# First mixer in another order: rotations and compression beside the attention gate's slots, a weight slot in each attention unit, pool output split, tanh gates

## The chip, the cores and the metric

One core of a Trainium2 chip. The metric is the device time of one execution in microseconds. The kernel before took 3319.39 us, the median of 3 runs (3317.85 to 3319.66).

## The reference, cut to what matters

Two transformer blocks on 256 tokens of width 2048, all in float32. The change is mostly in the first block's mixer:

```python
h = rmsnorm(x, norm_w)
proj = h @ w_in
(u_pool, g_pool, q, kc_raw, vc_raw, k_sel, v_sel, k_win, v_win, g_nsa, g_br) = split(proj)
y_pool = pool_mixer(u_pool, pool_mix, pool_scale) * silu(g_pool)   # causal means over 2, 4, 8, 16 tokens
y_a = y_pool @ w_pool_out
qh = rope(heads(q, 16), pos)
kc = rope(compress(heads(kc_raw, 4), pe_k, w1_k, w2_k), cmp_pos)   # 15 blocks of 32 tokens, stride 16:
vc = compress(heads(vc_raw, 4), pe_v, w1_v, w2_v)                  #   silu(block . w1) . w2, hidden 256
ksh, kwh = rope(heads(k_sel, 4), pos), rope(heads(k_win, 4), pos)
gates = sigmoid(g_br)
o_nsa = nsa_attention(qh, kc, vc, ksh, v_sel, kwh, v_win, gates)   # three softmaxes per head, gated, summed
y_b = (o_nsa * silu(g_nsa)) @ w_nsa_out
gm = sigmoid(h @ w_merge + b_merge)                                # 2 x 2048 wide
x = x + (gm[0] * y_a + gm[1] * y_b) @ w_out
```

The second block has its own input projection (with three narrow row projections ff, mi, mf), a forgetting attention, an mLSTM cell, an output projection and a PEER layer with 16384 experts, whose weights are most of what is loaded.

## The kernel before

**Weights as a stream of slots.** All large weights lie in one DRAM tensor `stream`, cut in slots of 128 x 2048 floats (1 MB). SyncE loads slot after slot into `raw[0]` and `raw[1]` in turn, each as soon as `raw_free` says that it may. A float32 product is made of three fp32r products: ScalarE rounds the slot, `whi <- raw` (`split`, L865), VectorE makes the rest, `wlo <- raw - whi` (L1343), which also frees `raw`, and TensorE multiplies whi by the high part of the activations (hTh), whi by the low part (hTl), and wlo by hTh. In `phase_t2` the first two are one matmul of 512 columns and VectorE adds the two halves as it reads the bank (`evac_t`, L1371); in `t_slot` (L431) there are 48 matmuls of 256 columns per slot; in `phase_n` (L497) 24 of 512 columns, and the tokens lie on partitions. A slot can be rounded only when the slot two before it has been multiplied (`slot_used`), and the split of slot n+1 runs under the matmuls of slot n. `phase(..., ahead=True)` also splits the first slot of what follows; elsewhere the next phase splits its first slot after its predecessor's last bank has been read.

**PHASES** gives the order of the stages in units of 4 slots: in_t 16 (u, g_pool, kc_raw, vc_raw, k_sel, k_win, q, g_nsa), in_n 2 (v_sel, v_win), narrow1 0.5 (g_br: 48 columns, stored 128 wide in one slot, and a dummy slot), cmp 2 (w1_k, w1_v), merge 8, pool_out 2, nsa_out 4, out1 4, then the second block.

**Between in_n and the attention** TensorE waits for both slots of narrow1, turns the gates, and then multiplies the cmp slots straight from `raw` in fp32 (L539, out 128 x 60, weights the stationary side, 256 matmuls in all). ScalarE takes the silus of g_pool and g_nsa at once (L944, L945) and swaps halves for the rotations (L952, L953), 12 pairs of heads; VectorE builds `kb` (L1423) and multiplies and adds the rotations (L1433 to L1435). GpSimd has pooled `u` during in_t (L1274 to L1290).

**The attention** has 32 units, u = 16 heads x 2 query blocks. TensorE's order is: turn(u) (L578, L580), scores(u+2) (L564 to L566), perhaps one t_slot of merge, values(u) (L589, L593). turn waits for VectorE's scaling (L1467), scores for ScalarE's copy of the turned probabilities (L982, L983), because both use banks 4 to 7. On VectorE: mask(u+1), scale(u), split. On ScalarE: exp(u+1) (L973, L974), copy(u), split, sigmoid of a merge bank (L992). Twenty of the 32 units have a slot (`MERGE_AT`); a sigmoid between exponentials has a table load on either side.

**After it**: the pooled groups are mixed (z, L621), 12 merge slots follow, then pool_out straight from `raw` in fp32 (L635, 16 matmuls per slot), gates on VectorE (L1521); before it the branch's 8 high parts (L1028) and low parts (L1514), 16 nsa_out slots with gate and sum (L1531, L1533), again 8 high and 8 low parts, and out1. `narrow2` (L506) in the second block is made like narrow1, followed by in2_v and in2_m.

## Time and profile before

| | us |
|---|---|
| median of 3 runs | 3319.39 |
| profiled execution | 3320.34 |
| its span | 3318.6 |
| matmul busy | 3073.2 |
| VectorE, ScalarE, GpSimd busy | 1758.4, 1244.0, 39.8 |

Loaded and written: 542.25 MB, 163 GB/s over the span. Mean granted TensorE clock 0.954. The page's chain of work that ended last is 82% TensorE, 11% VectorE and 5% ScalarE. The views used below are the page, tables of stretches, single rows of the timeline of one engine, groups of instructions by line, and the answer for one source line. Times are from the start of the span.

### The profile page before, as it was taken

To read this page: it belongs to the slowest core of one execution; us is meant where nothing else is said; L and a number is where in the kernel's file an instruction comes from. 1 tells how busy PE (TensorE), PEld (TensorE's weight loads), DVE (VectorE), ACT (ScalarE), POOL (GpSimd) and SP (SyncE) were. 2 spreads that over 40 slices of the span, in tenths; PEclk is the share of its full clock that TensorE was granted. 3 is DMA by queue.
4 is the path that set the end of the run, shared out by engine and by line. 5 is a ranking of instruction groups with operands and counts; after the bars stand their busy time and mean duration, and the time that the engine had idled before them with its cause. 6 is when DMAs were issued, how large, how long until landed. Compare 5 with 4: busy or idle time off the path is not lost.

```text
span 3318.6 us, 46264 instructions
## 1 busy us (share of the span) xinstructions
PE 3073.2 (93%) x18679; PEld 2750.7 (83%) x18679; DVE 1758.4 (53%) x2398; ACT 1244.0 (37%) x1352; POOL 39.8 (1%) x31
## 2 busy tenths in 40 slices
PE   6999998889998698995899999989999999999997
PEld 6888887778997587874689999988888999988885
DVE  4555453444244544566547988864445354444444
ACT  3333344444223333333334344434443333334443
POOL 0400000000000000000000000000000000000000
PEclk9999977989999898997999999999999999999998
DMA  4555543223454344431354445545555855545554
GB/s 178 187 181 188 177 152 115 77 77 115 153 185 160 123 177 152 153 127 64 139 181 165 174 165 171 164 158 190 190 191 194 276 185 182 184 164 191 190 190 152
DMA packets 89854, 542.25 MB, mean 163 GB/s; under 512 B 9264, under 2 KB 25648, under 8 KB 25904
## 3 DMA queue, kind: packets, MB, share of 16 engines
q1 hardware_dynamic: 71824, 522.33, 44.3%
q10 hardware_dynamic: 17952, 18.88, 1.7%
q8 instruction: 49, 0.80, 0.1%
q14 instruction: 29, 0.24, 0.0%
HBM read 530.68 MB, written 10.49 MB: 163 GB/s over the span
## 4 chain that ended last, share of the span: by engine, by line
PE 82%; DVE 11%; ACT 5%; issue 1%; DMA 0%; ACTq 0%; DVEq 0%; SPq 0%
PE bank L431 25%; PE bank L829 21%; PE bank L452 10%; PE bank L497 8%; PE bank L450 6%; DVE wlo L1343 4%; PE bank L473 3%; ACT whi L865 2%; PE bank L635 2%; PE bank L539 2%; DVE R L1883 1%; PE bank L449 1%; DVE R L1327 1%; PE bank L593 1%; PE bank L564 1%
## 5 line engine op out<-in xcount | busy, mean ns | idle before, releaser
L1343 DVE TENSOR_TENSOR wlo<-raw,whi 128x2048 fp32r<-128x2048 f32 x476 | 1090.0, 2291 | 796.9 <-ACT whi L865 795.6
L865 ACT ACTIVATE whi<-raw 128x2048 fp32r<-128x2048 f32 x476 | 908.2, 1910 | 1018.5 <-PE bank L452 368.2
L431 PE MATMUL bank<-hT,whi 128*128 128x256 f32 x5888 | 1116.3, 291 | 14.1 <-DVE wlo L1343 12.5
L431 PEld LDWEIGHTS bank<-hT,whi 128*128 128x128 f32 x5888 | 933.5, 196 | 18.4 <-issue 10.0
L431 PE MATMUL bank<-hT,wlo 128*128 128x256 f32 x2944 | 842.8, 286 | 0.0
L431 PEld LDWEIGHTS bank<-hT,wlo 128*128 128x128 f32 x2944 | 573.6, 195 | 0.0
L452 PE MATMUL bank<-hT,whi 128*128 128x512 f32 x1440 | 517.4, 401 | 0.0
L450 PE MATMUL bank<-hT,wlo 128*128 128x256 f32 x1536 | 418.8, 283 | 0.0
L452 PEld LDWEIGHTS bank<-hT,whi 128*128 128x128 f32 x1440 | 273.4, 190 | 63.5
L450 PEld LDWEIGHTS bank<-hT,wlo 128*128 128x128 f32 x1536 | 293.5, 191 | 8.2
L829 PE MATMUL bank<-whi,ghi 128*128 128x512 f32 x1024 | 281.7, 397 | 15.2 <-DVE wlo L1343 15.2
L829 PE MATMUL bank<-wlo,ghi 128*128 128x512 f32 x1024 | 276.2, 392 | 0.0
L829 PE MATMUL bank<-whi,glo 128*128 128x512 f32 x1024 | 275.0, 391 | 0.0
L497 PE MATMUL bank<-whi,hT 128*128 128x512 f32 x768 | 244.1, 399 | 25.8 <-DVE wlo L1343 25.8
L1340 DVE TENSOR_TENSOR glo<-R,ghi 128x256 fp32r<-128x256 f32 x128 | 54.5, 425 | 372.3 <-ACT whi L865 372.3
L829 PEld LDWEIGHTS bank<-whi,ghi 128*128 128x128 f32 x1024 | 187.6, 189 | 66.7 <-issue 15.2
L829 PEld LDWEIGHTS bank<-wlo,ghi 128*128 128x128 f32 x1024 | 193.5, 189 | 41.8
L829 PEld LDWEIGHTS bank<-whi,glo 128*128 128x128 f32 x1024 | 193.0, 188 | 40.8
L864 ACT ACTIVATE ghi<-R 128x256 fp32r x128 | 53.4, 418 | 419.9 <-PE bank L829 410.2
L497 PEld LDWEIGHTS bank<-whi,hT 128*128 128x128 f32 x768 | 148.4, 193 | 58.5 <-DVE wlo L1343 18.9
L497 PE MATMUL bank<-wlo,hT 128*128 128x512 f32 x384 | 152.9, 398 | 0.0
L815 PE MATMUL bank<-R 128*128 128x128 f32 x512 | 99.0, 275 | 2.8 <-DVE R L1883 2.5
(275 smaller groups left out, 2123.9 us busy)
## 6 DMA issues: line engine op xcount, KB each, us to landing
raw<-stream SPq DMA_DIRECT2D x492, 1024.0 KB, 4.8
gates_dram<-R ACTq DMA_DIRECT2D x64, 128.0 KB, 4.3
R<-gates_dram ACTq DMA_DIRECT2D x16, 512.0 KB, 5.3
xres<-x SPq DMA_DIRECT2D x1, 2048.0 KB, 7.7
out<-R SPq DMA_DIRECT2D x1, 2048.0 KB, 6.4
R<-mixw ACTq DMA_DIRECT2D x1, 1024.0 KB, 4.8
R<-fnw ACTq DMA_DIRECT2D x1, 1024.0 KB, 4.7
raw<-fnw SPq DMA_DIRECT2D x1, 1024.0 KB, 4.4
```

Source lines behind the costliest of these rows:

```text
L431: last = mm(bank[b][:, t * T:(t + 1) * T], w[t][:, ks], x_[:, k, :], start=(k == 0 and n == 0), stop=(k == KC - 1 and n == 2))
L450: last = mm(bank[s][:, 0:T], wlo[t][:, ks], hTh[:, k, :], start=False, stop=False)
L452: last = mm(*both, start=False, stop=(k == KC - 1))
L473: last = mm(bank[b][:], x_[:, k, ts_], w[t][:, kk * 512:(kk + 1) * 512], start=(k == 0 and n == 0), stop=(k == KC - 1 and n == 2))
L497: last = mm(bank[2 * h + b][:], x_[:, k, ts_], w[t][:, kk * 512:(kk + 1) * 512], start=(k == 0 and n == 0), stop=(k == KC - 1 and n == 2))
L539: last = mm(bank[4 + 2 * v + f][:, 0:NC4], raw[s % 2][:, ll * CH + f * P:ll * CH + (f + 1) * P], kb[v][:, l, :], start=(l == 0), stop=(l = ...
L635: last = mm(bank[s][:, e * T:(e + 1) * T], raw[t][:, (e * 8 + k) * P:(e * 8 + k + 1) * P], pT[:, U0 + k, :], start=(k == 0), stop=(k == 7))
L815: last = mm(bank[4 + (2 * s + q) % 4][:, c * P:(c + 1) * P], second_hot[:, k // 2, :], first_hot[:, k // 2, :], start=True, stop=True)
L829: last = mm(bank[4 * b + c][:], x_[:, t, ts_], w[t][:, c * 512:(c + 1) * 512], start=(first and s == 0 and n == 0), stop=(last_group and s ...
L865: A(whi[t][:], raw[t][:], ACT.Copy).then_inc(hi_ready[t], 1)
L1340: V.tensor_tensor(glo[:, t, :].rearrange("p (g o t) -> p g o t", o=1, t=4), gate_block(i * 4 + s, 1), ghi[:, t, :].bitcast(F32).rearrange( ...
L1343: V.tensor_tensor(wlo[t][:], raw[t][:], whi[t][:].bitcast(F32), ALU.subtract).then_inc(raw_free[t], 1)
```

## The change

- The order of the stream: in_t has only kc_raw, vc_raw, k_sel, k_win and q (32 slots); then in_n, narrow1, **gn** (g_nsa, 16 slots in the t2 form), **in_u** (u and g_pool, 16 slots in the t form), merge and the rest. The compression weights leave the stream for a tensor `cmpw`, which ScalarE loads in 8 transfers into a part of R that is free until in_u.
- `kb` is built beside in_n; the compression's products have the block rows as stationary side and the weights as moving side (8 matmuls of 256 columns per `hidden_slot`), placed in in_n, behind narrow1 and beside gn; the result is turned afterwards. The rotations, the gates' turn and sigmoid, and kc and vc are placed beside gn's 16 slots as well.
- `BESIDE` lists in_u's 16 slots and merge's; 4 run behind the first scores, then one in each of the 32 units. `MERGE_AT` is gone. g_nsa's silu is taken in four parts beside gn, g_pool's after the attention. GpSimd pools `u` one 256-token row block at a time while the attention runs.
- Merge's gates: sigmoid(z) is written as (1 + tanh(z/2)) / 2; the bias is halved once, the +1 joins the product, and the 0.5 the residual sum of out1.
- pool_out is split like the others (48 matmuls of 256 columns per slot); y's high and low parts are made in 4 pieces (in the place of hTh, hTl, first halves), the branch parts 8 to 15 beside it, 0 to 7 after it; nsa_out's first four slots take the k chunks in the order 8..15, 0..7 and wait piece by piece; so does out1.
- narrow1 and narrow2 come as two halves of the depth, each a slot with short splits. The first slot of in_n, narrow1, gn, in_u, pool_out, nsa_out, out1, narrow2, in2_v, in2_m and peer_u0 is split ahead.

The diff, cut to its core:

```diff
-PHASES = [("in_t", 16), ("in_n", 2), ("narrow1", 0.5), ("cmp", 2), ("merge", 8), ("pool_out", 2), ("nsa_out", 4),
+PHASES = [("in_t", 8), ("in_n", 2), ("narrow1", 0.5), ("gn", 4), ("in_u", 4), ("merge", 8), ("pool_out", 2), ("nsa_out", 4),
...
-MERGE_AT = [n * HQ * TB // (RING * MERGE_EARLY) for n in range(RING * MERGE_EARLY)]
+BESIDE = [("in_u", i, s) for i in range(4) for s in range(RING)] + [("merge", i, s) for i in range(8) for s in range(RING)]
+BESIDE_FIRST = 4
+BRANCH_ORDER = (*range(8, 16), *range(8))
+HIDDEN_AT = (1, 2, 4, 5, 7, 8)
...
@@ TensorE
+            def narrow(name, dst):
+                n = NARROW[name]
+                for t in range(2):
+                    pe.wait_ge(raw_free[t], consumed(name, 0, t))
+                    for kk in range(KC // 2):
+                        k, ks = t * KC // 2 + kk, slice(kk * n, (kk + 1) * n)
+                        for m, (w, x_) in enumerate(((whi, hTh), (whi, hTl), (wlo, hTh))):
+                            last = mm(dst, w[t][:, ks], x_[:, k, :],
+                                      start=(k == 0 and m == 0), stop=(k == KC - 1 and m == 2))
+                    last.then_inc(slot_used[t], 1)
...
+            def hidden_slot(n):
+                v, s = divmod(n, RING)
+                pe.wait_ge(kb_ready, v + 1)
+                pe.wait_ge(cw_full[n % 2], 16 * (n // 2 + 1))
+                for ll in range(8):
+                    l = 8 * s + ll
+                    last = mm(bank[6 + v][0:NC4, 0:CH], kb[v][:, l, :], cw[n % 2][:, ll * CH:(ll + 1) * CH],
+                              start=(l == 0), stop=(l == CB - 1))
+                last.then_inc(cw_used[n % 2], 1)
...
+            phase_n("in_n", lambda: hidden_slot(0))
+            narrow("narrow1", bank[5][0:48, 0:T])
+            hidden_slot(1)
+            for n in range(4 * RING):
+                t2_slot("gn", *divmod(n, RING))
+                if n == 0:
+                    pe.wait_ge(gbr_copied, 1)
...
+                if n in HIDDEN_AT:
+                    hidden_slot(2 + HIDDEN_AT.index(n))
+                if n == 3:
                     pe.wait_ge(gates_ready, 1)
+                    turn_hidden(0)
+                if n == 4:
+                    compressed_keys()
+                if n == 9:
+                    turn_hidden(1)
+                if n == 10:
+                    compressed_values()
...
             nsa_scores(0)
             nsa_scores(1)
+            for n in range(BESIDE_FIRST):
+                t_slot(*BESIDE[n])
...
             for u in range(units):
                 nsa_turn(u)
                 if u + 2 < units:
                     nsa_scores(u + 2)
-                if u in MERGE_AT:
-                    t_slot("merge", *divmod(MERGE_AT.index(u), RING))
+                t_slot(*BESIDE[BESIDE_FIRST + u])
                 nsa_values(u)
...
+            for n in range(2 * RING):
+                i, s = divmod(n, RING)
+                t = s % 2
+                pe.wait_ge(bank_free[s], i + B0["pool_out"][s])
+                pe.wait_ge(raw_free[t], consumed("pool_out", i, s))
+                for e in range(2):
+                    for k in range(8):
+                        pe.wait_ge(y_split, k // 2 + 1)
+                        ks = slice((e * 8 + k) * P, (e * 8 + k + 1) * P)
+                        for m, (w, y) in enumerate(((whi, y_hi), (whi, y_lo), (wlo, y_hi))):
+                            last = mm(bank[s][:, e * T:(e + 1) * T], w[t][:, ks], y[:, k, :],
+                                      start=(k == 0 and m == 0), stop=(k == 7 and m == 2))
+                last.then_inc(slot_used[t], 1)
+            for s in range(RING):
+                t_slot("nsa_out", 0, s, order=BRANCH_ORDER, ready=lambda n: pe.wait_ge(branch_split, n // 2 + 1))
+            phase_t("nsa_out", 1)
+            phase_n("out1", ready=lambda s: pe.wait_ge(branch_split, 8 + 2 * (s + 1)))
...
@@ ScalarE
+            def load_hidden(n):
+                if n >= 2:
+                    act.wait_ge(cw_used[n % 2], n // 2)
+                act.dma_start(cw[n % 2], cmpw[n]).then_inc(cw_full[n % 2], 16)
...
+            for n in range(4 * RING):
+                if n + 1 < 4 * RING:
+                    split("gn", *divmod(n + 1, RING))
+                else:
+                    split(*BESIDE[0])
+                if n < 12:
+                    swap_halves(n)
+                if n in (0, 2, 3, 5, 6):
+                    load_hidden((3, 4, 5, 6, 7)[(0, 2, 3, 5, 6).index(n)])
...
-                    last = A(R[:, bass.ds(at * T + 16 * T, T)], bank[b][:, e * T:(e + 1) * T], ACT.Sigmoid,
-                             bias=par[:, bass.ds(at + bm, 1)])
+                    last = A(R[:, bass.ds(at * T + 16 * T, T)], bank[b][:, e * T:(e + 1) * T], ACT.Tanh,
+                             bias=par[:, bass.ds(at + bm, 1)], scale=0.5)
...
+            split(*BESIDE[1])
+            nsa_exp(0)
+            for n in range(2, BESIDE_FIRST + 1):
+                split(*BESIDE[n])
+                beside_evac(n - 2)
             for u in range(units):
+                n = BESIDE_FIRST + u
                 if u + 1 < units:
                     nsa_exp(u + 1)
                 nsa_copy(u)
+                split(*BESIDE[n + 1])
+                beside_evac(n - 1)
...
@@ VectorE
+            for n in range(4 * RING):
+                if n + 1 < 4 * RING:
+                    split("gn", *divmod(n + 1, RING))
+                else:
+                    split(*BESIDE[0])
+                if n > 0:
+                    evac_one("gn", *divmod(n - 1, RING), GN0)
+                if n < 12:
+                    rope(n)
...
+            for n in range(2 * RING):
+                if n + 1 < 2 * RING:
+                    split("pool_out", *divmod(n + 1, RING))
+                else:
+                    split("nsa_out", 0, 0)
+                if 0 < n < 5:
+                    branch_low_part(n - 1, 3 + n, pT[:, GN0:GN0 + 16, :])
+                if n > 0:
+                    gate_pool(n - 1)
```

## Rows read from the trace of the kernel before

**Rows 1.** The page, part 1: busy us (share of the span) xinstructions.

```profile
PE 3073.2 (93%) x18679; PEld 2750.7 (83%) x18679; DVE 1758.4 (53%) x2398; ACT 1244.0 (37%) x1352; POOL 39.8 (1%) x31
```

**Rows 2.** Table by stretches: us; PE, PEld, DVE, ACT, POOL busy; PEclk, DMA, GB/s.

```profile
443.30:517.00 73.70, 66.26 (x326) 64.10 (x326) 35.85 (x58) 29.98 (x43) 0.00 (x0) 0.56 0.40 143
517.00:793.60 276.60, 231.73 (x1535) 211.79 (x1536) 126.97 (x356) 131.64 (x316) 0.00 (x0) 0.89 0.24 84
869.70:928.60 58.90, 55.49 (x259) 48.59 (x257) 12.73 (x17) 6.90 (x11) 0.00 (x0) 1.00 0.38 137
1022.50:1120.70 98.20, 89.62 (x384) 73.69 (x384) 46.90 (x33) 34.72 (x24) 0.00 (x0) 0.95 0.48 171
1247.00:1313.60 66.60, 54.24 (x241) 45.18 (x241) 31.95 (x30) 26.39 (x20) 0.00 (x0) 0.91 0.43 158
```

**Rows 3.** ScalarE's timeline (start, us, instruction, [idle before, releaser]): in_t, in_n, merge.

```profile
214.36 1.92 ACT L865 ACTIVATE whi<-raw 128x2048 fp32r<-128x2048 f32 x1 [3.73 <-PE bank L452]
...
416.15 1.92 ACT L865 ACTIVATE whi<-raw 128x2048 fp32r<-128x2048 f32 x1 [3.52 <-PE bank L497]
...
812.40 1.91 ACT L865 ACTIVATE whi<-raw 128x2048 fp32r<-128x2048 f32 x1 [3.85 <-PE bank L431]
```

**Rows 4.** VectorE's timeline: the multiplication behind one pool_out slot.

```profile
890.77 0.69 DVE L1521 TENSOR_TENSOR R<-bank,R 128x512 f32 x1 [6.21 <-PE bank L635]
```

**Rows 5.** ScalarE's copies, TensorE's scores (timelines); the turns (lines by form, 517.0 to 793.6).

```profile
607.37 0.60 ACT L982 ACTIVATE R<-bank 128x512 f32<-128x512 f32 x1 [4.67 <-PE bank L580]
...
617.20 0.38 ACT L982 ACTIVATE R<-bank 128x256 f32<-128x256 f32 x1 [1.53 <-PE bank L580]
...
769.72 0.38 ACT L982 ACTIVATE R<-bank 128x256 f32<-128x256 f32 x1 [3.11 <-PE bank L580]
...
778.67 0.60 ACT L982 ACTIVATE R<-bank 128x512 f32<-128x512 f32 x1 [1.95 <-PE bank L580]
...
770.39 0.46 PE L564 MATMUL bank<-R 128*128 128x128 f32 x2 [0.71 <-ACT R L983]
...
L578 PE MATMUL bank<-par,R 128*128 128x128 f32 x96 | 16.6, 283 | 18.7 <-DVE R L1467 18.7
```

**Rows 6.** Timelines of VectorE and TensorE in unit 10: scaling and turn.

```profile
614.96 0.23 DVE L1467 SCALAR_TENSOR_TENSOR R<-R,st,par 128x15 f32<-128x15 f32 x1
...
616.67 0.38 PE L578 MATMUL bank<-par,R 128*128 128x128 f32 x2
```

**Rows 7.** TensorE's timeline at the starts of six stages; VectorE's at 871.

```profile
398.08 0.76 PE L497 MATMUL bank<-whi,hT 128*128 128x512 f32 x1 [3.07 <-DVE wlo L1343]
...
928.57 0.50 PE L431 MATMUL bank<-hT,whi 128*128 128x256 f32 x2 [3.41 <-DVE wlo L1343]
...
1030.99 0.80 PE L497 MATMUL bank<-whi,hT 128*128 128x512 f32 x1 [8.53 <-DVE wlo L1343]
...
1249.98 0.45 PE L506 MATMUL bank<-hT,whi 128*68 128x256 f32 x2 [2.98 <-DVE wlo L1343]
...
1261.84 0.77 PE L497 MATMUL bank<-whi,hT 128*128 128x512 f32 x1 [4.47 <-DVE wlo L1343]
...
1313.56 0.55 PE L431 MATMUL bank<-hT,whi 128*128 128x256 f32 x1 [4.90 <-DVE wlo L1343]
...
871.42 4.91 DVE L1514 TENSOR_TENSOR hT<-R,hT 128x512 fp32r<-128x512 f32 x8 [8.71 <-ACT hT L1028]
```

**Rows 8.** Line L431 (ns min/median/max), splits at 79 to 121 and 121 to 163, the page's loads.

```profile
L431 PE MATMUL bank<-hT,whi x640: 277/283/562, 527.8 to 789.5; 128*128 128x256 f32 x160
...
L1343 DVE TENSOR_TENSOR wlo<-raw,whi 128x2048 fp32r<-128x2048 f32 x8 | 19.1, 2393 | 19.2 <-ACT whi L865 19.2
...
L1343 DVE TENSOR_TENSOR wlo<-raw,whi 128x2048 fp32r<-128x2048 f32 x8 | 18.3, 2292 | 20.0 <-ACT whi L865 20.0
...
raw<-stream SPq DMA_DIRECT2D x492, 1024.0 KB, 4.8
```

More of the change, by code:

```diff
@@ L129, in split_pairs @@
         out[name] = at
-        at += 0 if name in RAW else int(2 * n)
+        at += int(2 * n)
     return out
 def fills_per_bank(name, n):
-    if name in ("in_t", "in2_t", "wq"):
+    if name in ("in_t", "gn", "in2_t", "wq"):
         return (n,) * 4
-    if name in ("merge", "nsa_out", "in2_m", "in2_n", "peer_u0", "peer_u1"):
+    if name in ("in_u", "merge", "nsa_out", "in2_m", "in2_n", "peer_u0", "peer_u1"):
         return (n, n, 0, 0)
@@ L420, in turn_norm, with t_slot @@
                         last.then_inc(turned, 1)
-            def t_slot(name, i, s, between=None):
+            def t_slot(name, i, s, between=None, order=range(KC), ready=None):
                 b, t = s // 2, s % 2
@@ L427, in t_slot @@
                 pe.wait_ge(raw_free[t], consumed(name, i, s))
-                for k in range(KC):
+                for at, k in enumerate(order):
+                    if ready is not None:
+                        ready(at)
                     ks = slice(k * P, (k + 1) * P)
@@ L646, in _ @@
             phase_t2("in2_t")
-            narrow("narrow2", bank[5][0:ROW_AT[2] + MH, 0:T], ROW_AT[2] + MH, rowsT_ready)
+            narrow("narrow2", bank[5][0:NARROW["narrow2"], 0:T])
             phase_n("in2_v")
@@ L924, in phase_n @@
                             between(g)
+                if ahead is not None:
+                    split(ahead, 0, 0)
                 if dst is not None:
@@ L1044, in _ @@
             high_parts(1)
-            evac_t("in2_t")
-            split("narrow2", 0, 0)
+            phase("in2_t", keep, ahead="narrow2")
             split("narrow2", 0, 1)
+            split("in2_v", 0, 0)
             def gate_rows(g):
@@ L1150, in _ @@
             high_parts(3)
-            evac_t("wq")
-            split("peer_u0", 0, 0)
+            phase("wq", keep, ahead="peer_u0")
             for f in range(8):
@@ L1390, in phase_n, with evac_n @@
                             between(g, s)
+                if ahead is not None:
+                    split(ahead, 0, 0)
                 evac(n - 1)
-            def evac_n(name, dst, between=None):
+            def evac_n(name, dst, between=None, ahead=None):
                 def evac(g):
@@ L1481, in _ @@
             dve.wait_ge(gates_ready, 1)
-            dve.wait_ge(silu_done, 2)
-            split("merge", 0, 0)
+            split(*BESIDE[1])
             nsa_mask(0)
+            for n in range(2, BESIDE_FIRST + 1):
+                split(*BESIDE[n])
             for u in range(units):
@@ new lines, in _ @@
+            for n in range(2 * RING):
+                if n + 1 < 2 * RING:
+                    split("pool_out", *divmod(n + 1, RING))
+                else:
+                    split("nsa_out", 0, 0)
+                if 0 < n < 5:
+                    branch_low_part(n - 1, 3 + n, pT[:, GN0:GN0 + 16, :])
+                if n > 0:
+                    gate_pool(n - 1)
+            dve.wait_ge(slot_used[1], multiplied("pool_out", 1, 3))
+            for j in range(4):
+                branch_low_part(4 + j, j, pT[:, GN0:GN0 + 16, :])
@@ L1549, in _ @@
             norm(1, "norm2", 2)
-            evac_t("in2_t")
-            split("narrow2", 0, 0)
+            evac_t("in2_t", "narrow2")
             split("narrow2", 0, 1)
+            split("in2_v", 0, 0)
             def convolve(j):
```

472 lines of the change are left out of this document (254 added, 218 removed).

## The prediction

> **What bounds the kernel now.** The page's first part comes first: TensorE is busy 93% of the span, VectorE 53%, ScalarE 37%, GpSimd 39.8 us in all [rows 1]. So time is gained only where TensorE stands idle, runs work that could be cheaper, or runs at the lower clock. The second view is a table by stretches [rows 2]. It shows where that is in the part that the change touches. 443.3 to 517.0 (gates, rotations, compression; no weight slot multiplied) lasts 73.7 us at a granted clock of 0.56. The attention units, 517.0 to 793.6, last 276.6 us with 231.7 us of matmul at a clock of 0.89. The pool output takes 58.9 us, out1 with the wait before it 98.2, the narrow gates and in2_v of the second block 66.6. Third, ScalarE's own rows give the rhythm of a slot, since its next rounding starts when a slot has been multiplied: 1.92 + 3.73 = 5.65 us for an in_t slot, 1.92 + 3.52 = 5.44 for an in_n slot, 1.91 + 3.85 = 5.76 for a merge slot [rows 3]. Last, the idle times in front of TensorE's first matmul of a stage [rows 7].
>
> **Part 1: the front, up to the first scores.** Before, that moment is 517.0 us [rows 2].
> - in_t falls from 64 slots to 32. The row at 214.36 is the rounding that the end of the 32nd slot releases, so in_t now ends there [rows 3]. In_n follows without the 3.07 us gap [rows 7], since its first slot is split ahead: 8 x 5.44 = 43.5.
> - narrow1 in two halves: 48 matmuls of 256 columns, as in a merge slot, so 5.8. Its second half has a short split, done under the first.
> - Compression: 8 hidden_slot calls of 8 plain fp32 matmuls of 256 columns each. The nearest row is pool_out, 16 such matmuls per slot and 0.69 + 6.21 = 6.90 us between two multiplications of VectorE, which TensorE releases [rows 4]: 0.43 us each, 3.45 per call, 27.6 in all. Not below 2 us a call unless 60 weight columns load faster than 128 and that is what binds; not above 3.45.
> - gn: 16 x 5.65 = 90.4. Between the slots stand turns and the two small products; I take 3.5 us.
> - Do rotations fit beside gn? All that VectorE did in the 73.7 us stretch is 35.9 us [rows 2]; with 16 splits and reductions of 2.3 + 0.7 that is 84 us, in a stretch that now lasts over 114 us. ScalarE: 30.0 + 16 x 1.9 = 60. Each slot's order (split, reduction, rotation) leaves VectorE free about 0.6 us before it is needed. So nothing is added, and only 0.7 us a slot is spare where no hidden_slot follows.
> Sum: 214.4 + 43.5 + 5.8 + 27.6 + 90.4 + 3.5 = 385.2. Gain 131.8.
> The cmp weights no longer go through SP's queue but as 8 loads of 1 MB from ScalarE's. A load of that size takes 4.8 us from issue to landing [rows 8]. Each is issued one hidden_slot or more before it is used, behind ScalarE's split, and delays it by the issue alone. SP's next slot load has some 7 us before it is wanted (5.65 x 2 less the split), so a load twice as slow by sharing would stall 0 to 3 us. I take 0; the rest is a rival.
>
> **Part 2: the attention.** Two scores, 2.3 us; then 4 in_u slots, 4 x 5.76 = 23.0. nsa_mask(1) now queues on VectorE behind the split of the fifth slot, which cannot start before the third slot is multiplied, so unit 0's turn comes about 1.8 us late (1.9 rounding, 2.3 split, 1.8 mask, 1.0 scale, less a slot of 5.76, and the copy behind it).
> Then 32 units, each with a slot. ScalarE's copy of a unit's transposed probabilities marks the period: 617.20 - 607.37 = 9.83 us and 778.67 - 769.72 = 8.95 us, two units whose slot ran at full clock, an odd and an even one [rows 5]. A pair is 18.78 us, 16 pairs 300.5, less 3 for the last two units, which issue no scores. Units without a slot waited for VectorE's scaling (18.7 us over the stretch); with one they don't, only the 0.71 (or 0.92) us for ScalarE's copy is left [rows 5]. Is VectorE in time in every unit? Unit 10's scaling ends at 614.96 + 0.23 = 615.19 and its turn starts at 616.67 [rows 6]: 1.5 us to spare, and the order on both engines stays the same. The tanh gates drop two table loads per bank, on an engine that was idle then: nothing. The Trainium skill, page ScalarE: Activation LUTs, section Table sets, lists tanh in the set of exp; no row here shows a tanh.
> Sum: 2.3 + 23.0 + 1.8 + 300.5 - 3 = 324.6 against 276.6: costs 48.0. Parts 1 and 2 together gain 83.8.
> The pool pass moves beside the attention: 8 rounds of half the width on GpSimd, at most about 50 us from the 39.8, ended in unit 15 or so; z waits for it much later. Silu of g_pool (1.3 load, 1.9) comes before y, under z's 7 us. Merge's last 12 slots are unchanged.
> GpSimd beside VectorE: in 79 to 121 us, where the pool pass ran, the split averaged 2.393 us, after it 2.292 [rows 8]. 0.1 us per slot is inside the 1.5 us to spare, so 0. The Trainium skill, page SBUF — State Buffer, section Who interferes with whom, has VectorE's operations on two SBUF inputs and GpSimd's taking turns at an exclusive port; the trace shows a tenth of a microsecond per split. Were every GpSimd operation waited for in full, the sum would be 40 us higher.
>
> **Part 3: pool_out as split slots.** 58.9 before, with the 3.41 us gap [rows 2, 7]. Now: y_high and y_low start after the last merge gate, 0.8 + 0.6 + 0.6 and handovers = 2.3 us idle; 8 x 5.76 = 46.1; the branch parts (0.6 us each on either engine [rows 7]) lie between splits; at its end four high and four low parts and gate_pool delay nsa_out's second split by 0.7; the idle time costs clock as well: a mean of 0.95 over the 98.2 us around out1, behind 8.53 idle, is 4.9 us of work lost to the lower level [rows 2, 7], so in proportion 2.3 / 8.53 x 4.9 = 1.3. 50.4, gain 8.5. The 16 nsa_out slots stay at 5.76.
>
> **Part 4: into out1.** 98.2 before, with 8.53 idle [rows 2, 7]. out1's first slot is split already; TensorE waits only for two low parts: 1.6 for the last merge, 2 x 0.6, handover = 3.0. The second slot's split queues behind all eight low parts (8 x 0.61) and comes 0.5 late. 3.0 + 0.5 + 16 x 5.44 + 1.7 of lower clock (3.0 / 8.53 x 4.9) = 92.2, gain 6.0. The scale of 0.5 rides on an operation of the same width.
>
> **Part 5: the second block.** narrow2 and in2_v had 2.98, 4.47 and 4.90 us of idle time [rows 7], 66.6 in all [rows 2]. Now 5.8 for the halves; in2_v's first split starts when the first half is done, 2.9 + 1.9 + 2.3 = 7.1, so 1.3 idle; 43.5; in2_m's first slot is ready, its second queues behind VectorE's gate rows: 1.4. 52.0, gain 14.6. peer_u0's early split: TensorE had no gap there, 0.
>
> **Sum.** 83.8 + 8.5 + 6.0 + 14.6 = 112.9. The profiled execution took 3320.34 us (span 3318.6); 3320.3 - 112.9 = 3207.4. The median of the runs shown is 0.95 lower, so 3206.5; I forecast 3207.
>
> **Rivals.**
> - **The clock sinks in the units as it does now.** Granted 0.89 over 276.6 us [rows 2] means the lower level for 22% of it; there a matmul takes up to 562 ns against 283 [rows 8]. Over 325 us that is 36 us: 3243. For it: the 0.7 to 0.9 us waits remain. Against: the drops follow units without a slot. 10%.
> - **A slot in every unit eats the 1.5 us to spare**, by the evacuations now in each second unit, or hidden_slot or rotation work late by 1 us a time: 32 x 1 = 32, 3239. 8%. That the work isn't hidden as the change says is the far end of this one.
> - **The loads from ScalarE's queue collide with the stream**: 8 x 2.4 to 4.8, 19 to 38 us, 3226 to 3245. The busy share of the DMA engines beside in_t is near half. 8%.
> - **The port** (above), every GpSimd operation waited for: 3247. 3%.
> - **Cheaper than priced**: hidden_slot at 2 us (-12), half of the entry waits of 1.8, 2.3, 3.0, 1.3, 1.4 gone (-5): 3190 to 3197. 9%.
> - **Slower than before: the lower clock stays.** The units' TensorE work comes in groups with two waits in each; if the chip never grants the full clock there, the 325 us double. With a share x of that work at half speed the loss is 325 x, and from x = 0.35 on it eats the 113 us; the whole would give 3532. Before it is at 0.22 with 12 units of 32 without a slot. 2%.
>
> **How the numbers follow.** The forecast has 60% (3199 to 3217: 0.3 us either way on each of some 30 handovers); the rivals 10, 8, 8, 3, 9 and 2. The range runs from the cheap case to the clock case, 3192 to 3243. A change of under 0.2% (6.6 us) could not be told from none by a measurement of this kernel: for faster 97%, within 1%, slower 2%.
>
> **What the profile after would show.** First scores near 385 us and the last unit near 710; in gn, matmuls of a slot every 5.65 us with 3.4 us of fp32 between; the stretch of the units at a clock above 0.97 and no idle time put down to VectorE's scaling; idle before pool_out 2 to 2.5, before out1 about 3, around in2_v 1.3 and 1.4. Idle time in gn put down to a DMA would speak for the collision; one in the units put down to the line of the scaling, for the lost 1.5 us. The prediction is wrong if the units' period is not 9.4 us on average or hidden_slot is not near 3.4.

## The result, and the profile after

The changed kernel took 3205.91 us, the median of 4 runs (3205.14 to 3209.21); the kernel before, beside it on the same chip, 3318.62 (3317.7 to 3319.66). The ratio is 0.9662, 95% interval 0.9648 to 0.9676. The profiled execution took 3205.14 us with a span of 3202.9; granted clock 0.976 over the whole, before it was 0.954. One of the four runs of `v2c_other_cycle` below took 3768.71 us, at a granted clock of 0.742 against 0.974 to 0.976 in the others, and is left out of its median.

The page, part 1, answers to [rows 1]: TensorE does 70 us less in a span 116 us shorter.

```profile
PE 3003.4 (94%) x18939; PEld 2689.7 (84%) x18939; DVE 1767.4 (55%) x2395; ACT 1235.7 (39%) x1356; POOL 39.6 (1%) x57
```

The table by stretches answers to [rows 2]: up to the first scores, the four slots behind them, the 32 units, the pool output, out1 with its wait, narrow2 and in2_v (us; PE, PEld, DVE, ACT, POOL busy; PEclk, DMA, GB/s).

```profile
31.00:387.50 356.50, 356.03 (x1930) 297.38 (x1931) 191.09 (x164) 131.21 (x98) 0.00 (x0) 0.99 0.54 195
387.50:413.80 26.30, 24.99 (x205) 24.64 (x204) 13.42 (x20) 12.39 (x17) 0.00 (x0) 1.00 0.59 215
413.80:712.60 298.80, 274.01 (x2097) 256.27 (x2098) 154.30 (x352) 127.35 (x307) 39.43 (x53) 0.99 0.32 112
...
789.20:844.40 55.20, 52.07 (x432) 51.89 (x432) 32.81 (x29) 24.95 (x24) 0.00 (x0) 1.00 0.49 171
...
931.00:1022.80 91.80, 88.99 (x385) 73.18 (x384) 44.64 (x31) 32.90 (x23) 0.00 (x0) 0.98 0.50 183
...
1148.80:1200.00 51.20, 49.52 (x241) 41.59 (x240) 27.49 (x26) 22.29 (x17) 0.00 (x0) 1.00 0.53 188
```

The stretch at clock 0.56 is gone, and the units run at 0.99 where they had 0.89. TensorE's timeline at the starts of the stages answers to [rows 7]: pool output, nsa_out's second slot, out1, in2_v.

```profile
791.55 0.47 PE L685 MATMUL bank<-hT,whi 128*128 128x256 f32 x2 [2.37 <-DVE hT L1657]
...
844.40 0.50 PE L446 MATMUL bank<-hT,whi 128*128 128x256 f32 x2 [0.79 <-DVE wlo L1464]
...
933.86 0.47 PE L520 MATMUL bank<-whi,hT 128*128 128x512 f32 x1 [2.80 <-DVE hT L1664]
...
1156.29 0.47 PE L520 MATMUL bank<-whi,hT 128*128 128x512 f32 x1 [1.68 <-DVE wlo L1464]
```

Before, 3.41, 8.53, 2.98, 4.47 and 4.90 us stood there; in2_m's first slot (1200.02) follows without a gap. In the front, ScalarE's roundings beside gn answer to [rows 3]:

```profile
332.72 1.91 ACT L916 ACTIVATE whi<-raw 128x2048 fp32r<-128x2048 f32 x1 [2.35 <-PE bank L465]
...
342.06 1.91 ACT L916 ACTIVATE whi<-raw 128x2048 fp32r<-128x2048 f32 x1 [6.14 <-PE bank L465]
...
365.21 1.92 ACT L916 ACTIVATE whi<-raw 128x2048 fp32r<-128x2048 f32 x1 [3.88 <-PE bank L465]
370.86 1.92 ACT L916 ACTIVATE whi<-raw 128x2048 fp32r<-128x2048 f32 x1 [3.73 <-PE bank L465]
```

It is 5.65 us without (370.86 - 365.21) and 9.34 us with a hidden_slot between two slots (342.06 - 332.72). TensorE has no idle time put down to a DMA here. ScalarE has 0.85 us of it, once, in front of its rounding at 268.78, and TensorE does not wait for that one. The new loads land in 5.0 us (the page's part on DMA issues, [rows 8]):

```profile
R<-cmpw ACTq DMA_DIRECT2D x8, 1024.0 KB, 5.0
```

In the units, ScalarE's copies (timeline, first fence) and TensorE's waits (lines by form, 413 to 713, second fence) answer to [rows 5]:

```profile
567.05 0.38 ACT L1076 ACTIVATE R<-bank 128x256 f32<-128x256 f32 x1 [1.53 <-PE bank L628]
...
585.85 0.38 ACT L1076 ACTIVATE R<-bank 128x256 f32<-128x256 f32 x1 [1.53 <-PE bank L628]
```

```profile
L626 PE MATMUL bank<-par,R 128*128 128x128 f32 x96 | 15.9, 275 | 1.6 <-DVE R L1611 1.6
...
L612 PE MATMUL bank<-R 128*128 128x256 f32 x30 | 10.1, 417 | 13.9 <-ACT R L1077 13.9
...
L612 PE MATMUL bank<-R 128*128 128x128 f32 x30 | 6.9, 311 | 10.7 <-ACT R L1077 10.7
```

Lines L626, L612 and L446 of after are L578, L564 and L431 of before. A pair of units takes 585.85 - 567.05 = 18.80 us. The wait for VectorE's scaling, 18.7 us before, is 1.6, of which 1.34 is the first turn (at 413.83). What is left is the wait for ScalarE's copy, 13.9 + 10.7 = 24.6 us.

Where the 115.7 us of span went, from the starts of the stages in both timelines: front 129.5, attention -48.9, pool output 9.6 (the 0.79 of nsa_out's second slot counted to it), nsa_out 1.3, out1 6.5, in2_t 0.3, narrow2 and in2_v 15.4, in2_m 2.2 (14.22 to 12.00 us for its two slots), and -0.2 in all the rest.

### The profile page after: what moved, and what is told of

Its sections match the earlier page's. It is cut to its first block, busy times and chain, and to the rows that moved or that the text cites. A ratio compares the mean times of both kernels' runs of the same rounds, so it can differ in the third digit from the quotient of the medians.

```text
span 3202.9 us, 46654 instructions
## 1 busy us (share of the span) xinstructions
PE 3003.4 (94%) x18939; PEld 2689.7 (84%) x18939; DVE 1767.4 (55%) x2395; ACT 1235.7 (39%) x1356; POOL 39.6 (1%) x57
## 4 chain that ended last, share of the span: by engine, by line
PE 83%; DVE 10%; ACT 4%; issue 2%; DMA 0%; ACTq 0%; DVEq 0%; SPq 0%
PE bank L446 28%; PE bank L879 22%; PE bank L465 9%; PE bank L520 8%; PE bank L463 5%; DVE wlo L1464 4%; PE bank L492 3%; ACT whi L916 2%; PE bank L685 1%; PE bank L551 1%; DVE R L2049 1%; PE bank L641 1%; PE bank L462 1%; DVE R L1447 1%; PE bank L612 1%
## 5 line engine op out<-in xcount | busy, mean ns | idle before, releaser
L1464 DVE TENSOR_TENSOR wlo<-raw,whi 128x2048 fp32r<-128x2048 f32 (+1 forms) x484 | 1102.0, 2277 | 831.2 <-ACT whi L916 829.9
L916 ACT ACTIVATE whi<-raw 128x2048 fp32r<-128x2048 f32 (+1 forms) x484 | 918.3, 1898 | 930.7 <-PE bank L446 374.4
L446 PE MATMUL bank<-hT,whi 128*128 128x256 f32 x6400 | 1191.8, 287 | 6.7 <-DVE wlo L1464 5.0
L446 PEld LDWEIGHTS bank<-hT,whi 128*128 128x128 f32 x6400 | 996.7, 192 | 10.7 <-DVE wlo L1464 5.5
L446 PE MATMUL bank<-hT,wlo 128*128 128x256 f32 x3200 | 905.8, 283 | 0.0
L446 PEld LDWEIGHTS bank<-hT,wlo 128*128 128x128 f32 x3200 | 613.4, 192 | 0.0
L465 PE MATMUL bank<-hT,whi 128*128 128x512 f32 x1200 | 431.2, 401 | 0.0
L465 PEld LDWEIGHTS bank<-hT,whi 128*128 128x128 f32 x1200 | 227.9, 190 | 52.7
L463 PEld LDWEIGHTS bank<-hT,wlo 128*128 128x128 f32 x1280 | 244.9, 191 | 6.4
```

What stands on the lines that cost most here:

```text
L446: last = mm(bank[b][:, t * T:(t + 1) * T], w[t][:, ks], x_[:, k, :], start=(at == 0 and n == 0), stop=(at == KC - 1 and n == 2))
L463: last = mm(bank[s][:, 0:T], wlo[t][:, ks], hTh[:, k, :], start=False, stop=False)
L465: last = mm(*both, start=False, stop=(k == KC - 1))
L916: A(whi[t][:, 0:w], raw[t][:, 0:w], ACT.Copy).then_inc(hi_ready[t], 1)
L1464: V.tensor_tensor(wlo[t][:, 0:w], raw[t][:, 0:w], whi[t][:, 0:w].bitcast(F32), ALU.subtract).then_inc(raw_free[t], 1)
```

## Experiments

Each is a change to the kernel after; ratios are to the kernel before on the same chip. "Later" and "+" count from 3205.91.

**The small parts, each undone alone.** `e1_block2_as_before`:

```diff
-                w = 8 * NARROW[name] if name in NARROW else SLOT
+                w = 8 * NARROW[name] if name == "narrow1" else SLOT
...
-            phase("in2_t", keep, ahead="narrow2")
+            phase("in2_t", keep)
+            split("narrow2", 0, 0)
             split("narrow2", 0, 1)
-            split("in2_v", 0, 0)
...
-            phase_n("in2_v", vN2, gate_rows, started=True, ahead="in2_m")
+            phase_n("in2_v", vN2, gate_rows)
```

> The changed kernel with part 5 undone: the splits of narrow2 are full wide again and no first slot of narrow2, in2_v and in2_m is split ahead (the two halves of the depth stay). By the forecast's steps part 5 is worth 14.6 us (narrow2, in2_v and in2_m with their idle times went from 66.6 to an expected 52.0, and the trace after has 51.2), so this takes 3218 to 3221 us, with idle times near 3, 4.5 and 4.9 us back in front of narrow2, in2_v and in2_m. Rival: the stages only wait later for the gate rows, which are not touched, and less than 5 us come back (under 3211).

Measured: 3221.78 us, ratio 0.9698 (0.9682 to 0.9714). TensorE's timeline has waits at the three old places again; the second is 3.01 us where 4.47 stood, because the two halves stay:

```profile
1152.71 0.45 PE L532 MATMUL bank<-hT,whi 128*68 128x256 f32 x2 [2.98 <-DVE wlo L1465]
...
1163.12 0.50 PE L520 MATMUL bank<-whi,hT 128*128 128x512 f32 x1 [3.01 <-DVE wlo L1465]
...
1213.51 0.76 PE L446 MATMUL bank<-hT,whi 128*128 128x256 f32 x2 [4.90 <-DVE wlo L1465]
```

From narrow2's start to in2_m's it is 60.80 us (1213.51 - 1152.71) and 2.98 ahead of it, against 51.18 in after: 12.6 us. In2_m's two slots take 13.7 us instead of 11.9, at a granted clock of 0.82 in their first 12.3 us instead of 1.00, so the trace accounts for 14.3 us. The ratios give 12, the medians 15.9.

`e2_pool_out_fp32`, the pool output straight from `raw` again, with all eight branch parts ahead of it:

```diff
                 for e in range(2):
                     for k in range(8):
-                        pe.wait_ge(y_split, k // 2 + 1)
-                        ks = slice((e * 8 + k) * P, (e * 8 + k + 1) * P)
-                        for m, (w, y) in enumerate(((whi, y_hi), (whi, y_lo), (wlo, y_hi))):
-                            last = mm(bank[s][:, e * T:(e + 1) * T], w[t][:, ks], y[:, k, :],
...
+                        last = mm(bank[s][:, e * T:(e + 1) * T], raw[t][:, (e * 8 + k) * P:(e * 8 + k + 1) * P],
+                                  pT[:, U0 + k, :], start=(k == 0), stop=(k == 7))
...
```

> The changed kernel with part 3 undone: pool_out multiplied in plain fp32 straight from raw, all eight branch parts before it, nsa_out's first slot not split ahead. Part 3 was forecast at 8.5 us; the trace after has 48.5 from the last merge slot to nsa_out and 0.8 behind it, against 58.9, so I expect 9 to 11 us more: 3215 to 3217. Rival: the gain of that stretch came from the full clock in nsa_out rather than from the cheaper products, then pool_out itself is no longer here than 50 and the time rises by under 5.

Measured: 3215.73 us, ratio 0.9680 (0.9664 to 0.9696). TensorE's pool output lasts from 789.64 to 845.06, 55.4 us against 46.3, with 3.30 us behind it (its timeline, nsa_out's first matmul):

```profile
848.36 0.51 PE L447 MATMUL bank<-hT,whi 128*128 128x256 f32 x2 [3.30 <-DVE wlo L1451]
```

9.8 us by the medians, 6 by the ratios. Three fp32r passes from split weights are cheaper here than one fp32 matmul from `raw`.

`e8_out1_as_before`:

```diff
-            phase_n("out1", ready=lambda s: pe.wait_ge(branch_split, 8 + 2 * (s + 1)))
+            pe.wait_ge(branch_split, 16)
+            phase_n("out1")
...
-            phase("nsa_out", keep, started=True, ahead="out1")
+            phase("nsa_out", keep, started=True)
```

> The changed kernel with part 4 undone: out1 waits for all eight branch parts and its first slot is split after them. Forecast 6.0 us, so 3211 to 3213, with 8.5 us of idle time in front of out1. Rival: the last low part decides anyway and less than 2 us return.

Measured: 3210.56 us, ratio 0.9672 (0.9656 to 0.9689). The medians differ by 4.7 us, the ratios by 3, and the two ratios' intervals overlap; what shows the part is the trace. The old wait is back (TensorE's timeline) and out1 ends 5.3 us later:

```profile
938.75 0.79 PE L520 MATMUL bank<-whi,hT 128*128 128x512 f32 x1 [8.53 <-DVE wlo L1465]
```

**The cover of the rotations.** `e10_rotations_behind_gn` takes the 12 exchanges and rotations out of gn's slots and puts them behind gn's last slot:

```diff
-                if n < 12:
-                    swap_halves(n)
...
             silu_gn(3)
+            for j in range(12):
+                swap_halves(j)
...
-                if n < 12:
-                    rope(n)
...
             evac_one("gn", 3, 3, GN0)
+            for j in range(12):
+                rope(j)
```

> The changed kernel with the 12 swaps and rotations moved from beside the 16 gn slots to behind them, in front of the first scores. In the kernel before a rotation took 1.93 us and nothing else ran. If gn is bound by TensorE alone, as forecast, its 16 slots keep their 5.65 us, 12 x 1.93 + 1.5 = 25 us of idle time come before the first scores and 3 to 5 us of lower clock behind them: 3233 to 3237. Rival: beside gn VectorE was late anyway, part of it comes back in gn, under 3226.

Measured: 3232.76 us, ratio 0.9742 (0.9726 to 0.9759), 26.9 us later. VectorE's last rotation and TensorE's first scores (a timeline each):

```profile
412.52 0.69 DVE L1567 TENSOR_TENSOR R<-R 128x512 f32<-128x512 f32 x1
```

```profile
413.27 0.80 PE L612 MATMUL bank<-R 128*128 128x128 f32 x2 [26.52 <-DVE R L1567]
```

The scores start 413.27 - 387.54 = 25.7 us later. So of the front's 129.5 us about 26 come from this cover alone; it had been costed at nothing beside gn, and it is nothing there.

**A slot in every unit.** `e3_twenty_units` gives 20 of the 32 units a slot and puts the other 12 behind:

```diff
-MERGE_EARLY = 5
+MERGE_EARLY = 2
+SLOT_AT = [n * HQ * TB // 20 for n in range(20)]
...
-                t_slot(*BESIDE[BESIDE_FIRST + u])
+                if u in SLOT_AT:
+                    t_slot(*BESIDE[BESIDE_FIRST + SLOT_AT.index(u)])
```

> The changed kernel, but only 20 of the 32 units have a slot (the kernel before's places), and 12 merge slots more run behind the attention. Forecast's theory: a slot in a unit covers the wait for VectorE's scaling (1.3 us) and keeps the clock up. Twelve slots behind cost 12 x 5.76 = 69.1; the units without one shrink by 5.93 and get 1.3 of wait: with the clock at its full level the stretch would be 298.8 - 12 x 4.6 = 243 and the whole 3220; if the clock sinks as in the kernel before, the stretch is near that kernel's, 272, and the whole near 3249. So near 3249 says that the clock is worth twice the waits, 3220 that it is the waits alone, under 3211 that neither matters.

Measured: 3245.88 us, ratio 0.9772 (0.9756 to 0.9788), 40.0 us later. The stretch of the units (table), their turns (lines by form), and one turn of a unit without a slot (timeline), a fence each:

```profile
413.80:690.00 276.20, 234.77 (x1557) 213.85 (x1557) 129.31 (x347) 106.18 (x285) 35.52 (x53) 0.89 0.23 83
```

```profile
L627 PE MATMUL bank<-par,R 128*128 128x128 f32 x96 | 17.1, 288 | 17.4 <-DVE R L1614 17.4
```

```profile
673.01 0.44 PE L627 MATMUL bank<-par,R 128*128 128x128 f32 x2 [1.30 <-DVE R L1614]
```

Clock 0.89 and 17.4 us of waiting for the scaling: both are the values of before ([rows 2, 5]: 0.89, 18.7), with everything else new. It is the units without a slot that brought them: TensorE has nothing to do there while VectorE scales. With the clock at its full level 3220 was expected, and 3249 with it sunk as before; so by that estimate some 26 of the 40.0 us go with the clock.

**How much VectorE has to spare per unit.** `e4a_dve_1us_per_unit` and `e4b_dve_2us_per_unit` put a reduction that nobody reads behind each unit's split, of 1024 (1.21 us) and 2048 elements (2.28 us):

```diff
                 split(*BESIDE[BESIDE_FIRST + u + 1])
+                V.tensor_reduce(st[:, 240:241], xres[:, 0, 0:1024], AX.X, ALU.max)
```

> The changed kernel with one more VectorE reduction of 1024 elements (some 1.2 us) in each of the 32 units, between the split and the mask. The forecast said that VectorE is 1.5 us early for each turn (rows of unit 10). Then 1.2 us a unit cost nothing: 3205 to 3210. Rival: no time to spare (the port, the evacuations): 32 x 1.2 = 38, 3244.

> The same with 2048 elements (some 2.3 us). With 1.5 us to spare 0.8 us a unit show: 26 us, 3232, and idle time of TensorE put down to VectorE's scaling. If nothing was spare: 32 x 2.3 = 74, 3280; if far more was, 3206.

Measured: 3211.46 us, ratio 0.9676 (0.9660 to 0.9692), and 3239.4 us, ratio 0.9759 (0.9743 to 0.9775). The turns in lines by form, e4a (413 to 730) and then e4b (395 to 760, since its units end at 746.7):

```profile
L626 PE MATMUL bank<-par,R 128*128 128x128 f32 x96 | 16.3, 280 | 4.0 <-DVE R L1611 3.9
```

```profile
L626 PE MATMUL bank<-par,R 128*128 128x128 f32 x96 | 17.8, 296 | 21.9 <-DVE R L1611 21.9
```

With 1.21 us more the turns wait 4.0 us in all, with 2.28 us more 21.9. In e4b's timeline the waits from 513 us on are 0.60 to 0.74, but for the last, 1.22 (before that up to 2.53), so the spare time is about 2.28 - 0.7 = 1.6 us. The 33.5 us that e4b costs are more than its 20.3 us of further idle time. The rest is matmul time, 3017.8 us instead of 3003.4 (the pages), and the granted clock in the units is 0.96 instead of 0.99 (0.88 instead of 0.98 from 413.8 to 500, tables of both). How much of it is the clock, and how much each wait costs by itself, this pair of runs does not separate; the kernel v2 below gives the price of a wait at the full clock.

**Tanh and the port.** `e5_sigmoid_gates`, one word (it leaves out the right gate values, and only its time is used):

```diff
-                    last = A(R[:, bass.ds(at * T + 16 * T, T)], bank[b][:, e * T:(e + 1) * T], ACT.Tanh,
+                    last = A(R[:, bass.ds(at * T + 16 * T, T)], bank[b][:, e * T:(e + 1) * T], ACT.Sigmoid,
```

> The changed kernel with Sigmoid in the place of Tanh in merge's gates (so the gates' values are not the reference's: 1 + sigmoid(z/2) instead of 1 + tanh(z/2)); it brings the table loads of 1.28 us back on either side of each of 10 gates between units. Forecast: tanh gained nothing, ScalarE has time: 3205 to 3208. Rival: the loads delay the exponentials, hence the scaling and the turn: 10 x (2.6 - 1.5) = 11 or more, 3217 and up.

Measured: 3203.31 us, ratio 0.9653 (0.9637 to 0.9669). ScalarE's timeline shows the pair of table loads around a gate:

```profile
641.80 1.28 ACT L1086 ACT_TABLE_LOAD   x1
...
643.95 1.28 ACT L1067 ACT_TABLE_LOAD   x1
```

They are there, 1.28 us each, and cost nothing that can be measured: the ratio's interval holds that of after.

`e6_pool_three_times` runs GpSimd's pass three times:

```diff
-                step(nc.gpsimd.tensor_copy(bufs[0][:, PAD:], u))
-                a, s = 0, 1
+                for _ in range(3):
+                    step(nc.gpsimd.tensor_copy(bufs[0][:, PAD:], u))
+                    a, s = 0, 1
...
```

> The changed kernel with GpSimd doing the copy, the sums and the scaling of its pool pass three times over for every row block (same result; some 80 us more of GpSimd beside the attention, ended before the attention is). By the traces a split beside the pass averages about 0.1 us longer (2.38 against 2.29) and VectorE has over 1 us to spare in a unit: 3205 to 3208. Rival, the exclusive port, every further GpSimd operation waited for in full: up to 80 us more, 3285; if only what exceeds the spare time shows, 10 to 20.

Measured: 3204.11 us, ratio 0.9647 (0.9631 to 0.9663). The time does not change. GpSimd is busy 96.1 us instead of 39.6 (page, part 1), and the turns wait 2.5 us instead of 1.6 (second fence, lines by form, 413 to 730):

```profile
PE 3005.2 (94%) x18939; PEld 2692.0 (84%) x18939; DVE 1772.1 (55%) x2395; ACT 1235.7 (39%) x1356; POOL 96.1 (3%) x129
```

```profile
L626 PE MATMUL bank<-par,R 128*128 128x128 f32 x96 | 15.9, 275 | 2.5 <-DVE R L1611 2.5
```

That is not because the two engines never meet. In after, GpSimd's and VectorE's timelines (a fence each):

```profile
457.06 1.34 POOL L1399 COPY R<-R 128x256 f32<-128x256 f32 x1
...
461.21 0.40 POOL L1399 COPY R<-R 128x256 f32<-128x256 f32 x1
```

```profile
455.86 2.29 DVE L1464 TENSOR_TENSOR wlo<-raw,whi 128x2048 fp32r<-128x2048 f32 x1 [4.38 <-ACT whi L916]
...
465.03 2.61 DVE L1464 TENSOR_TENSOR wlo<-raw,whi 128x2048 fp32r<-128x2048 f32 x1 [3.85 <-ACT whi L916]
```

A copy of GpSimd that takes 0.40 us alone takes 1.34 when it starts inside a split, and ends at 458.40, just behind the split's end at 458.15; in e6 one at 511.12 takes 2.35 beside the split that starts at 510.51. The split at 465.03 starts 0.15 us behind a GpSimd addition of 0.61 us and takes 0.32 longer. So these two do take turns, the one that is first runs on, and most of the price falls on GpSimd, which has time.

**What the 24.6 us of waiting for ScalarE's copy are worth.** The scores of unit u+2 write the banks from which ScalarE copies the turned probabilities of unit u. `v2_slot_before_scores` puts the slot between the turn and the scores, and VectorE's scaling one unit ahead, so that the next turn is ready. Both are changed at once:

```diff
                 nsa_turn(u)
+                t_slot(*BESIDE[BESIDE_FIRST + u])
                 if u + 2 < units:
                     nsa_scores(u + 2)
-                t_slot(*BESIDE[BESIDE_FIRST + u])
...
             nsa_mask(0)
+            nsa_scale(0)
...
                     nsa_mask(u + 1)
-                nsa_scale(u)
+                    nsa_scale(u + 1)
```

> A version of the changed kernel meant to be faster: in each unit TensorE does the weight slot before the scores of u+2 (turn, slot, scores, values), and VectorE masks and scales unit u+1 before the split. The 0.71 and 0.92 us that scores wait for ScalarE's copy (13.9 + 10.7 us in the trace after) then lie under the slot, and unit 0 no longer waits 1.3 us for mask(1). The chain scores, mask, exp, scale (1.7 + 1.5 + 1.1 us and handovers) has a whole unit of 8.6 us. Expected 3206 - 25.9 = 3180. Rival: VectorE or ScalarE is late for the split of the next slot, and the time is the same or higher (3200 to 3220).

Measured: 3168.25 us (3165.57 to 3168.85), ratio 0.9535 (0.9519 to 0.9550): faster than both kernels, 37.7 us below after by the medians, 42 by the ratios, where 25.9 were expected. The units in a table, and ScalarE's copies (timeline):

```profile
413.80:675.00 261.20, 261.20 (x2092) 254.27 (x2091) 158.89 (x352) 124.70 (x309) 41.24 (x53) 1.00 0.37 130
```

```profile
546.65 0.36 ACT L1076 ACTIVATE R<-bank 128x256 f32<-128x256 f32 x1
...
563.14 0.36 ACT L1076 ACTIVATE R<-bank 128x256 f32<-128x256 f32 x1
```

TensorE is busy for 261.20 of 261.20 us, and a pair takes 16.49 us instead of 18.80. The wait was longer than its idle time. TensorE's timelines, after and then v2, from a turn to what follows it:

```profile
566.52 0.38 PE L626 MATMUL bank<-par,R 128*128 128x128 f32 x2
...
567.73 0.46 PE L612 MATMUL bank<-R 128*128 128x128 f32 x2 [0.71 <-ACT R L1077]
```

```profile
544.86 0.38 PE L626 MATMUL bank<-par,R 128*128 128x128 f32 x2
...
545.10 0.36 PE L446 MATMUL bank<-hT,whi 128*128 128x256 f32 x1
```

567.73 - 566.52 = 1.21 us against 0.24: 0.97 us saved for 0.71 of idle time. The group that follows is another one in v2, so the pair is the safer measure: 18.80 - 16.49 = 2.31 us saved for 0.71 + 0.92 = 1.63 of idle time, with the granted clock at 1.00 in both (500 to 600, tables). Where nothing has to be waited for, the records of two groups overlap (545.07 + 0.27 is behind 545.10 in v2's timeline); a wait loses that overlap, which is the likely reason.

**Is it VectorE's load, or the order?** `v2_dve_2us_per_unit` is that kernel with the 2048-element reduction behind each split (`st[:, 240 + u:241 + u]` as its target, otherwise as in e4b).

> The faster version (slot before scores) with the reduction of 2048 elements (2.3 us) in every unit, which cost the changed kernel 33 us. In this order VectorE's chain should have 3 us or more to spare for each turn, so 0 to 3 us over the version without it, a ratio to the kernel before of 0.954 to 0.955. Rival: its 37 us came at the price of all spare time, then 30 to 70 us are added, 0.963 and up.

Measured: 3214.64 us, ratio 0.9680 (0.9664 to 0.9696), 46.4 us above v2. The expectation was wrong. TensorE waits 30.8 us for VectorE's splits (lines by form, 413 to 714), though VectorE is busy for 218.5 us of 298.8 and ScalarE for 121.9 (table):

```profile
L446 PE MATMUL bank<-hT,whi 128*128 128x256 f32 x999 | 186.6, 288 | 30.8 <-DVE wlo L1464 30.8
```

```profile
413.80:712.60 298.80, 266.45 (x2032) 250.54 (x2031) 218.53 (x379) 121.94 (x299) 39.39 (x53) 0.99 0.31 107
```

VectorE's timeline, then ScalarE's, over one unit:

```profile
504.15 2.29 DVE L1464 TENSOR_TENSOR wlo<-raw,whi 128x2048 fp32r<-128x2048 f32 x1 [1.40 <-ACT whi L916]
506.36 2.28 DVE L1637 TENSOR_REDUCE st<-xres 128x1 f32<-128x2048 f32 x1
...
508.88 0.68 DVE L1594 TENSOR_TENSOR R<-bank,par 128x512 f32<-128x512 f32 x1
...
514.31 2.29 DVE L1464 TENSOR_TENSOR wlo<-raw,whi 128x2048 fp32r<-128x2048 f32 x1 [1.05 <-ACT whi L916]
```

```profile
510.68 0.51 ACT L1067 ACTIVATE R<-R,st 128x256 f32<-128x256 f32 x1 [6.56 <-DVE st L1600]
...
512.39 1.89 ACT L916 ACTIVATE whi<-raw 128x2048 fp32r<-128x2048 f32 x1
```

Each starts where the one before ends: split 504.15, reduction 506.36 (then nsa_out's 0.42, once in a pair), mask 508.88, exponential 510.68, rounding 512.39, split 514.31. That is a closed chain of 10.16 us through two engines, both of which are idle for part of it. The next unit, without nsa_out, takes 9.30 from split to split, so a pair takes 19.46 us where TensorE needs 16.49; over 16 pairs that is 47.5 us, for 46.4 measured. The rounding hangs on the mask only because ScalarE does exponential, copy, rounding in this order. `v2c_other_cycle` has the same instructions (the diff is against `v2_dve_2us_per_unit`), on ScalarE as copy, rounding, exponential and on VectorE as mask, split, scale, reduction:

```diff
-                if u + 1 < units:
-                    nsa_exp(u + 1)
                 nsa_copy(u)
                 split(*BESIDE[n + 1])
+                if u + 1 < units:
+                    nsa_exp(u + 1)
                 beside_evac(n - 1)
...
                 if u + 1 < units:
                     nsa_mask(u + 1)
-                    nsa_scale(u + 1)
                 split(*BESIDE[BESIDE_FIRST + u + 1])
+                if u + 1 < units:
+                    nsa_scale(u + 1)
```

> The kernel with slot before scores and 2.3 us more of VectorE work per unit (ratio 0.9680), with the same instructions in another order: on ScalarE copy, rounding, exponential instead of exponential, copy, rounding; on VectorE mask, split, scale, the added reduction instead of mask, scale, split, the added reduction. Nothing is added or left out but the reduction, whose result nobody reads. Theory (the 46 us were a cycle: mask, exponential, copy, rounding, split, added reduction, mask followed each other on two engines in one unit, about 10 us against a period of 8.25): in the new order the exponential runs beside the split, so the chain of a unit is copy 0.8, rounding 1.9, split or exponential 2.3, scale 1.0, about 6.3 us from the turn's end, and VectorE's own work is 7.7 us of 8.25. The 2.3 us then cost nearly nothing: ratio 0.954 to 0.957, TensorE's idle time in front of the scaling and the slots near zero. Rival (VectorE's load as such is what binds, 7.7 us of work in 8.25): the time stays near 3215, ratio 0.966 to 0.969. A value between would say that the handovers on VectorE cost a part of it.

Measured: 3168.62 us, ratio 0.9535 (0.9514 to 0.9556). The units in a table, and VectorE's splits in the timeline:

```profile
413.00:675.00 262.00, 262.00 (x2096) 254.85 (x2096) 224.08 (x385) 124.99 (x309) 40.44 (x53) 1.00 0.36 130
```

```profile
505.73 2.29 DVE L1464 TENSOR_TENSOR wlo<-raw,whi 128x2048 fp32r<-128x2048 f32 x1 [1.44 <-ACT whi L916]
...
508.89 2.28 DVE L1638 TENSOR_REDUCE st<-xres 128x1 f32<-128x2048 f32 x1
...
514.08 2.29 DVE L1464 TENSOR_TENSOR wlo<-raw,whi 128x2048 fp32r<-128x2048 f32 x1 [0.90 <-ACT whi L916]
```

VectorE is busy for 224 of 262 us and TensorE never waits: 2.28 us more of work per unit cost nothing that can be measured (the ratio is that of v2). It was the order, not the load. Which of the two exchanges, ScalarE's or VectorE's, would have been enough was not run.

## Why the prediction held, step by step

The forecast was 3207 us for a measured 3205.91; the steps sum to 112.9 us where 115.7 were found.

- **Front.** First scores at 387.5 instead of 385.2. The mis-sized term is hidden_slot: 9.34 - 5.65 = 3.69 us between two roundings, 3.60 from its first matmul to the next slot's in TensorE's timeline, instead of 3.45; 8 times, 1.2 to 1.9 of the 2.3 us. It lies above the upper bound that the prediction gave it (the 0.43 us per matmul left out the handovers around a call). The 3.5 us for turns and small products, which no row supported, were 4.0 to 4.5: gn took 116.5 us (271.04 to 387.54), less 90.4 for its slots and 6 hidden slots of 3.60 to 3.69. e10 shows that the rotations' cover is real: without it 26 us.
- **Attention.** 325.5 us instead of 324.6. Period of a pair 18.80 (18.78), wait at the entry 1.34 (1.8), 24.6 us left for the copy, 1.6 us to spare by e4b (1.5): each term held. The 32 units took 299.2 us for a forecast 297.5; from 415 to 418 the granted clock was 0.57, which is most of that. That the copy's waits were kept as they were is right as a forecast; that they were 37 us to be had, v2 shows.
- **Tanh and GpSimd at nothing.** e5: the loads come back on an engine that has time. In after, the splits next to the pool pass (430 to 500) take 2377 ns on average and later ones (560 to 690) 2292 (lines by form), 0.1 us as forecast, and in e6 a pass three times as long changes nothing. So the rival falls as it was stated, with every GpSimd operation waited for in full by VectorE. The taking turns itself is there: what the forecast did not say is that GpSimd does most of the waiting, up to 2 us at a time.
- **Pool output.** 49.3 us instead of 50.4. Wait 2.37 (2.3), slots 46.2 (46.1), nsa_out's second slot 0.79 (0.7). The term that failed is the 1.3 us of lower clock: behind 2.37 us of idle time the granted clock stayed 1.00. Nsa_out gained 1.3 us, which it had lost behind 3.41 us of idle time (0.98 over it before, 1.00 now).
- **Into out1.** 91.7 instead of 92.2: wait 2.80 (3.0), no wait at the second slot (0.5), a short stretch at the lower clock (0.57 from 934 to 938).
- **Second block.** 51.2 instead of 52.0. Wait before in2_v 1.68 (1.3); the 1.4 before in2_m's second slot did not come. in2_m itself gained 2.2 us that the sum had not: before, its first slots ran at a granted clock of 0.77 behind 4.90 us of idle time, now at 1.00.
- **Rivals.** The clock that sinks in the units: 0.99, and e3 shows the condition (units without a slot). The spare 1.5 us eaten: idle time by the scaling 1.6. The loads: landed in 5.0 us, TensorE has no idle time put down to them. Cheaper than priced: no, hidden_slot was dearer, and of the entry waits only the 1.4 was gone. Lower clock for good: no; and its "0.22" is the share of the time at the lower level, of the work it is 0.11 / 0.89 = 0.12, so the 0.35 was further off than the text says.

So the total is right partly because misses cancel: the front and the attention gave 2.3 and 0.9 us less than forecast, the stages behind them 1.1, 1.3, 0.5, 0.3, 0.8 and 2.2 more; most of the latter is clock that the old waits had cost in the stage behind them. The medians of e1, e2 and e8 give 15.9, 9.8 and 4.7 us for parts 5, 3 and 4, where the prediction had 14.6, 8.5 and 6.0. The ratios give 12, 6 and 3, each to about 5 us either way, so only e1's part is clear of the noise by times alone; the other two rest on the traces.

## What to carry to other kernels

Put independent work directly behind an instruction whose result must pass through another engine before TensorE may go on; moving a slot by one place, with the scaling a unit earlier, was worth 37 us here, a third of what the whole rewrite brought. To ask whether an engine can take more, don't add up its busy time: follow the longest closed chain through the engines' orders over one period, because an engine that is idle a quarter of the time can still be what a period waits for, and exchanging steps can open the chain. A wait costs more than its idle time, here about 1.4 times.
